# Tokens spread in pairs by products over half the rows, and inner products moved behind each search, in a PEER layer

## The reference, cut to what matters

```python
q = (x @ w_q).reshape(bsz, seq, 8, 2, 128)
s1 = einsum('bshd,hnd->bshn', q[..., 0, :], sub_k1)      # 128 scores for each token, head and half
s2 = einsum('bshd,hnd->bshn', q[..., 1, :], sub_k2)
v1, i1 = top_k(s1, 16); v2, i2 = top_k(s2, 16)
top_s, pos = top_k(all 256 sums v1 + v2, 16)             # 16 experts of 128*128, for each head
gates = softmax(top_s)
u = u_tab[experts]                                       # experts: 128 for each token
act = gelu(einsum('ced,cd->ce', u, x)) * gates
out = einsum('ce,ced->cd', act, v_tab[experts])
```

## Time and profile before

| | |
|---|---|
| median of three executions | 1939.52 us |
| profiled execution, its time / its span | 1947.71 / 1946.0 us |
| TensorE busy | 1806.9 us, 93% of the span |
| VectorE busy | 926.9 us, 48% |
| ScalarE busy, GpSimd busy | 432.9 us, 427.8 us (22% each) |
| moved by DMA | 620.29 MB, 319 GB/s over the span |
| TensorE's `spread_token` products in the window 1401.7 to 1619 | 192 |

### The profile page before, as it was taken

The page is one execution under the profiler, slowest core; times in us unless marked ns, Lnnn a source line. Parts: engine busy times, 40 slices in busy tenths (PEclk is TensorE's granted clock), DMA queues, the critical chain, the costliest instruction groups (busy, mean ns, idle before and its releaser), DMA issues. The chain is left out here.

```text
span 1946.0 us, 23689 instructions
## 1 busy us (share of the span) xinstructions
PE 1806.9 (93%) x9356; PEld 1190.3 (61%) x9356; DVE 926.9 (48%) x1988; ACT 432.9 (22%) x839; POOL 427.8 (22%) x312
## 2 busy tenths in 40 slices
PE   4989999988999999998899999979699999999998
PEld 4975444437787744442675548978588885444443
DVE  4467311123567731112798625966666662222222
ACT  5462111114345321111511424200100110000001
POOL 6820000015668400000300015112022121112110
PEclk7999899998999989999999999999899999999999
DMA  9886799994568589999432333699789999999996
GB/s 394 347 320 217 316 430 429 429 430 170 198 235 313 227 328 430 430 429 429 154 108 87 141 122 118 217 367 389 292 354 391 410 393 373 416 415 403 417 414 269
DMA packets 95089, 620.29 MB, mean 319 GB/s; under 512 B 11520, under 2 KB 12032, under 8 KB 60672
## 3 DMA queue, kind: packets, MB, share of 16 engines
q1 hardware_dynamic: 75824, 482.88, 62.5%
q0 software_dynamic: 18432, 134.23, 17.0%
q10 hardware_dynamic: 720, 1.61, 0.2%
HBM read 617.63 MB, written 1.05 MB: 318 GB/s over the span
## 5 line engine op out<-in xcount | busy, mean ns | idle before, releaser
L3038 PEld LDWEIGHTS bank<-peer_xT,peer_tiles_a 128*128 128x128 f32 x1376 | 160.3, 192 | 21.1 <-issue 12.5
L3038 PE MATMUL bank<-peer_xT,peer_tiles_a 128*128 128x128 f32 x1376 | 164.5, 276 | 6.7 <-DMA peer_tiles_a<-in_peer_u 4.6
L3087 PE MATMUL bank<-peer_tiles_a,peer_H 128*128 128x512 f32 x344 | 159.6, 602 | 6.2 <-DMA peer_tiles_a<-in_peer_v 4.2
L227 POOL TENSOR_TENSOR w_lo<-ring,w_hi 128x1024 fp32r<-128x1024 f32 x60 | 148.3, 2474 | 64.0 <-ACT w_hi L217 63.6
L3262 DVE CUSTOM_DVE_ANT_0 peer_junk<-peer_rows_b,bank 128x1024 bf16<-128x1024 f32 x64 | 78.1, 1220 | 166.8 <-issue 163.8
L1091 PE MATMUL bank<-ring,moe_slots 128*64 128x512 f32 x576 | 132.0, 609 | 9.7 <-DMA ring<-in_stream 9.7
L3058 PE MATMUL bank<-peer_x_rows_hi,peer_ident 128*128 128x512 f32 x256 | 130.6, 510 | 0.4 <-DVE peer_pre L3262 0.3
L3262 DVE CUSTOM_DVE_ANT_0 peer_junk<-peer_rows_a,bank 128x1024 bf16<-128x1024 f32 x48 | 58.6, 1220 | 123.6 <-issue 119.9
L3087 PEld LDWEIGHTS bank<-peer_tiles_a,peer_H 128*128 128x128 f32 x344 | 64.5, 191 | 82.6 <-issue 72.1
L3134 POOL DMA_INDIRECT peer_rows_a<-in_peer_uv,peer_index x48 | 45.5, 949 | 306.5 <-PE bank L3068 263.4
L3134 POOL DMA_INDIRECT peer_rows_b<-in_peer_uv,peer_index x64 | 60.3, 943 | 231.2 <-PE bank L3068 216.3
(11 more groups left out here) (518 smaller groups left out, 3591.6 us busy)
## 6 DMA issues: line engine op xcount, KB each, us to landing
ring<-in_stream SPq DMA_DIRECT2D x103, 2048.0 KB, 12.7
early<-in_stream SPq DMA_DIRECT2D x32, 2048.0 KB, 18.2
peer_tiles_a<-in_peer_u SPq DMA_DIRECT2D x86, 512.0 KB
peer_tiles_a<-in_peer_v SPq DMA_DIRECT2D x86, 512.0 KB
sb_mod_ring<-in_ada_t SPq DMA_DIRECT2D x64, 512.0 KB, 6.3
peer_tiles_b<-in_peer_u SPq DMA_DIRECT2D x42, 512.0 KB
peer_tiles_b<-in_peer_v SPq DMA_DIRECT2D x42, 512.0 KB
ret_mod_ring<-in_ada_t SPq DMA_DIRECT2D x32, 512.0 KB, 5.2
```

The lines of the kernel that those rows point to most:

```text
L227: pool.tensor_tensor(self.shaped(self.w_lo, q, by_columns), self.quarter(n, q, by_columns), self.shaped(self.w_hi, q, by_columns).bitcast( ...
L3038: last = pe.matmul(K.bank[:, 2 + n // 4 % 2, n % 4 * P:(n % 4 + 1) * P], u[:, k, :], xT[:, k, :], start=(k == 0), stop=(k == KD - 1))
L3087: last = pe.matmul(K.bank[:, 2 + dh, :], H[:, m, :], first.slot(n)[:, dh * 512:(dh + 1) * 512], start=(m == 0), stop=(m == PK - 1))
```

## The change

It does three things.

1. **Pairs.** `spread_token(i)` becomes `spread_pair(p)`, which spreads tokens 2p and 2p + 1 by eight products: each has 64 rows instead of 128 (the one-hot column and the token rows of one 64-row half), and the products of the two halves stand next to each other in the list and write different banks (4, 5 for one token, 6, 7 for the other). `token` is renumbered so that each pair has one token of each half.
2. **One set of banks.** A pair fills all of banks 4 to 7. So `spread_pair` waits until both `dot`s of the pair before are done; in the groups stretch each `gate_unit` waits for the `dot`s of the pair before it and the spread waits for `h_gated` of the units before it. The groups are written two at a time: 8 `keys`, 4 `gate_unit`s and 3 pairs.
3. **Places.** `pick_head` calls `dot_at` after each half and at its end, 24 places in all. From the sixth place (counted from 0: place 5) on, every second one runs two `dot`s. On TensorE the 20 tokens of this stretch stand after tiles 27, 30, ... 54 instead of 25, 27, ... 63. The exponential of the first tile (`PICKED_AT`) stands on ScalarE after tile 63 instead of tile 59.

```diff
-TOKENS_FROM = 24
-PICKED_AT = 59
+FIRST_TOKEN = 26
+PICKED_AT = 63
-BESIDE_PICKS = (EARLY - TOKENS_FROM) // 2
+BESIDE_PICKS = 20
+PAIR_AT = {FIRST_TOKEN + 1 + 3 * p: p for p in range(BESIDE_PICKS // 2)}
...
-    token = lambda i: P // QUAD * (i % QUAD) + i // QUAD
+    strip = lambda i: (0, 2, 1, 3)[i % QUAD]
+    token = lambda i: P // QUAD * strip(i) + i // QUAD
...
-            def spread_token(i):
-                if BESIDE_PICKS <= i <= VALUES_FROM + 1:
-                    pe.wait_ge(dotted, i)
-                elif i >= 2:
-                    pe.wait_ge(dotted, i - 1)
-                elif i == 1:
+            def spread_pair(p):
+                if p:
+                    pe.wait_ge(dotted, 2 * p)
+                else:
                     pe.wait_ge(index_made, 1)
-                one = first.ident[:, token(i):token(i) + 1].to_broadcast([P, P])
                 for dh in range(2):
                     for n, part in enumerate(first.x_rows):
-                        last = pe.matmul(K.bank[:, 4 + 2 * buffer_of(i) + dh, :], one, part[:, dh * 512:(dh + 1) * 512], start=(n == 0),
-                                         stop=(n == 1))
+                        for r in range(2):
+                            t, own = token(2 * p + r), slice(64 * r, 64 * (r + 1))
+                            last = pe.matmul(K.bank[:, 4 + 2 * r + dh, :], first.ident[own, t:t + 1].to_broadcast([64, P]),
+                                             part[own, dh * 512:(dh + 1) * 512], start=(n == 0), stop=(n == 1))
                 last.then_inc(spread, 1)
-                if i % QUAD == 1 and i > QUAD:
-                    values_of(i // QUAD - 1)
+
+            def weigh_pair(p):
+                if p % 2 == 0 and p:
+                    values_of(p // 2 - 1)
...
             def gate_unit(m):
                 pe.wait_ge(a_ready, m + 1)
                 pe.wait_ge(b_ready, m + 1)
+                pe.wait_ge(dotted, BESIDE_PICKS + 2 * (3 * (m // 4) + m % 4 // 2 + 1))
...
             turn_picks(0, 6)
+            pe.wait_ge(selT_made, 1)
+            for e in range(GROUPS_LEFT // 2):
+                n, m, p = EARLY + 8 * e, 4 * e, BESIDE_PICKS // 2 + 3 * e
+                spread_pair(p)
                 keys(n)
+                weigh_pair(p)
                 keys(n + 1)
+                gate_unit(m)
+                gate_unit(m + 1)
                 keys(n + 2)
+                pe.wait_ge(h_gated, m + 2)
+                spread_pair(p + 1)
...
             for m in range(PK):
-                for i in range(before_values(m), before_values(m + 1)):
-                    spread_token(VALUES_FROM + i)
+                for p in range(pairs_before(m), pairs_before(m + 1)):
+                    spread_pair(p)
                 values(m)
+                for p in range(pairs_before(m), pairs_before(m + 1)):
+                    weigh_pair(p)
...
+            def dot_at(place):
+                i = place + BESIDE_PICKS - 3 * PK_HEADS
+                if i > 0 and i % 2:
+                    dot(i - 1)
+                    dot(i)
```

More of the change, by code:

```diff
@@ L2963, in peer_stage, with pairs_before @@
     qT = S.first_tables[:].rearrange("p (h t) -> p h t", t=T)
-    def before_values(m):
-        return min(m * (TOKENS - VALUES_FROM) // (PK - 6), TOKENS - VALUES_FROM)
-    def buffer_of(i):
-        return 0 if BESIDE_PICKS <= i < VALUES_FROM else i % 2
+    def pairs_before(m):
+        return VALUES_FROM // 2 + min(m * ((TOKENS - VALUES_FROM) // 2) // (PK - 6), (TOKENS - VALUES_FROM) // 2)
     with nc.Block() as block:
@@ L3198, in _ @@
                     exponential(0)
-                if n % 2 == 1 and n > TOKENS_FROM:
-                    spread_walked((n - TOKENS_FROM) // 2)
-            for g in range(GROUPS_LEFT):
-                i = BESIDE_PICKS + 3 * g
-                spread_walked(i)
-                spread_walked(i + 1)
-                gelu(EARLY // 4 + g)
-                spread_walked(i + 2)
-            for i in range(VALUES_FROM, TOKENS):
-                spread_walked(i)
+                if n in PAIR_AT:
+                    pair_walked(PAIR_AT[n])
+            for e in range(GROUPS_LEFT // 2):
+                p = BESIDE_PICKS // 2 + 3 * e
+                pair_walked(p)
+                gelu(EARLY // 4 + 2 * e)
+                pair_walked(p + 1)
+                pair_walked(p + 2)
+                gelu(EARLY // 4 + 2 * e + 1)
+            for p in range(VALUES_FROM // 2, TOKENS // 2):
+                pair_walked(p)
             act.activation(warm[:], eps[:], ACT.Sqrt)
@@ L3225, in pick_head @@
                     top_sixteen(dve, c, val[:, half, :], idx[:, half, :], scores[:, tt, m * PK:(m + 1) * PK])
+                    dots_at(3 * h + half)
                 c.settle()
@@ L3306, in _ @@
             for h in range(PK_HEADS):
-                pick_head(0, h)
-                for i in range(max(h - 1, 0) * BESIDE_PICKS // (PK_HEADS - 1), h * BESIDE_PICKS // (PK_HEADS - 1)):
-                    dot(i)
+                pick_head(0, h, dot_at)
             recover(0)
```

70 lines of the change are left out of this document (37 added, 33 removed).

## The result

The changed kernel takes 1923.05 us in the median of four executions (1920.88 to 1923.89), the kernel before 1940.37 us in the median of four (1938.49 to 1945.17). The ratio is 0.9907, 95% interval 0.989 to 0.9925: a gain of about 17 us, 0.9%. The forecast was 1912.5 us, 27 us less, with a range of 1901 to 1930. The profiled execution took 1923.27 us, span 1921.6.

The account below looks back on a forecast made before the run. DMA at 416 GB/s was taken to bound late picks and nearly the values, TensorE the groups, with both idle at the gap. Gains of 8 (picks), 13 (groups) and 6 (values) sum to 27 us: 1939.5 to 1912.5, range 1901 to 1930.

Parts of the forecast that it names:

- The wait on the exponential: Before turn_picks: TensorE waits for gelu, table load, exponential, three small normalize steps and handovers, 3.4 us in all.
- 9 x 1.8 + 1.94 = 18.1: End of the picks: TensorE has nine tiles and a quad left from about 1372.0, until 1390.1.
- 1.20 forecast: Cost of a pair on TensorE: 0.96 us of side-by-side steps plus 0.24, against 2.04 for two tokens.
- The row on which the choice between rule and trace rested: Trace before: a 0.19 us weight load lies under a product on the same 128 rows, so loads were taken as hidden.
- I allow 0.75 us a round, 6 us: Groups: allowance for new waits of gates and pairs on VectorE, taken off the 20.4 us saving.
- Two groups ... After: 24.15 us: Groups: TensorE time for two groups falls from 26.7 to 24.15 us, 20.4 less in all.
- less stock left over from the groups takes 1.5: Values: less stock from the groups takes 1.5 us off the 7.5 us gain, leaving 6.
- some 15 us or more: Values: TensorE's added waits for peer_v tiles beyond the present ones, at 414 to 416 GB/s.
- Late gathers and waits eat the groups' gain: Rival: at 2.4 us of waits a round the groups gain nothing, time 1926; chance 0.13.
- The halves take turns: Rival: a pair takes 2.16 us, with 7 us of group waits, time 1950; chance 0.10 including loads that don't hide.
- DMA filled entirely: Rival: waits covered and stock sufficient, the 41 us bound is neared, time 1900; chance 0.07.
- the signs that were to show the forecast wrong: Pair over 1.6 us, TensorE waiting over 2 us a round for dotted or h_gated, values' DMA clearly below 410 GB/s.

Follow-up runs that it names:

- e1: Kernel before with only the new places (tokens after tiles 27, 30, ... 54, dot places, exponential after tile 63), spreads over 128 rows: 1935.31 us, ratio 0.9968.
- e5: Changed kernel with each of a pair's eight products over all 128 rows; places, waits and banks kept: 1934.99 us, ratio 0.9966.
- e10: Changed kernel with the exponential behind tile 59 and the groups' last quad summed ahead of the first v tile: 1921.47 us, ratio 0.9894.
- e8: Changed kernel with the last 30 pairs spread over 126 v tiles instead of 122: 1924.42 us, ratio 0.9921.
- e2: Changed kernel with the picks' old places (pairs after tiles 27, 31, ... 63, dots at ends of heads, exponential behind 59): 1932.15 us, ratio 0.9958.
- e3: Changed kernel with a pair's four products of one half issued before the four of the other: 1926.34 us, ratio 0.9921.
- e4: Changed kernel with the exponential back behind tile 59 instead of 63: 1920.79 us, ratio 0.9899.

## Why the prediction was right or wrong

The direction and the range were right, and the size was off: 17 us against 27. By the stretches 8 + 13 + 6 were forecast and 7.0 + 11.9 - 2.0 came.

**Picks: right in sum, with two errors that nearly cancel.** 8 forecast, 7.0 measured, and e1 shows that the places alone do it (6.6). The wait on the exponential was to be 3.4 us and is 3.35. TensorE ends its tiles at 1383.87, which is 120.0 us behind the first gather; forecast was 1390.1, 118.7 behind it. But the way there is another. The last pair ends 98.1 us behind the first gather instead of 100.6. The sum "9 x 1.8 + 1.94 = 18.1" counts a quad that isn't there: behind the last pair of the picks no quad falls due, the fifth one stands in the groups. And the nine tiles take 21.9 us, because TensorE waits for tiles three times, 1.64, 1.72 and 1.42 us, which the sum left out. So tiles that DMA brings set this end, and not TensorE's work; that the result is within 1.3 us is partly luck. Not forecast was the half clock behind so short a wait.

**The pair: 1.20 forecast, 1.12 on its own rows, and 1.39 with what it does to its neighbours.** A tile ahead of a pair takes 1.88 us, one ahead of a 128-row spread 1.71 (in e5 as in before); a tile behind a pair and ahead of a quad takes 1.98, behind a 128-row pair (e5) 1.88. So 0.17 us on the way in and 0.10 on the way out are paid in the tiles. I took the change of shape from the quad, whose 0.23 contains it, but counted it inside the pair's own steps, where only part of it is.

The row on which the choice between rule and trace rested held up. In after's timeline with weight loads a load for the lower part starts at 1401.52 and ends under the products that started at 1401.41 on the same rows:

```profile
1401.41 0.50 PE L3056 MATMUL bank<-peer_x_rows_hi,peer_ident 64*128 64x512 f32 x2
1401.52 0.19 PEld L3056 LDWEIGHTS bank<-peer_x_rows_lo,peer_ident 64*128 64x128 f32 x2
1401.74 0.39 PE L3056 MATMUL bank<-peer_x_rows_lo,peer_ident 64*128 64x512 f32 x2
```

The Trainium skill ("TensorE: Matmul & The Clock Gate", Part 3, The mechanism) says in one sentence that a load overlaps products in flight only when its row group differs. By that rule the pair would take 1.96 us; the trace shows 1.12, and the measurement decides. The same section, further up, also lets a load run ahead when it goes to the background weight buffer; this trace agrees with that, though it doesn't show where the load goes.

**Groups: nearly right in sum (13 and 11.9), with two errors that cancel.** The step "I allow 0.75 us a round, 6 us" for the new waits was wrong: TensorE shows none behind the first pair, and e5 with the same waits has the length of before. The step "Two groups ... After: 24.15 us" was too low by 0.78: a round takes 24.93. Of it the tiles are 1.90 instead of 1.80 on average (49.86 less six pairs of 1.12, eight gate units of 0.895 and three quads of 1.85 leaves 30.4 us for sixteen tiles), the gate units 0.895 instead of 0.81; pairs and quads are a little cheaper. I had read each kind in the one row where it was shortest, and the cost of coming back from another kind of product stands in the next tile. The half clock at the start of the stretch costs 2.2 us more (1388.74 to 1440.79 is 52.05 us for what later takes 49.86).

**Values: wrong, and this is the step that failed.** The prediction said that 124.6 MB at 416 GB/s take 299.5 instead of 307 us, 7.5 less, "less stock left over from the groups takes 1.5". Both halves of it fell: the 6 us of gain did not come.
- The 406 GB/s were not a rate a little too low all along, which a faster TensorE could have raised. They were 416 nearly throughout and three dips, the larger two at the entry and at the last slots. The faster TensorE left these two: 22.8 us of idle DMA in the stretch before, 22.1 after. The other profiles say the same: 20.3 and 20.2 in e1 and e5, which spread tokens over 128 rows, and 18.8 to 24.6 in the seven others with pairs and whole tiles of `v`. e10 moved the first dip without gain, e8 only moved some of the idle time at the end.
- The stock was worth more than 1.5. Groups and values move 208 MB together. The faster groups moved 1.0 MB less in their time, and the values had 1.1 MB more: 1.1 / 416 = 2.6 us. The same shows in e2, e3 and e8, whose groups moved 80.3 to 80.6 MB against 81.4 and 82.0 in e1 and e5.

Together -2.6 + 0.7 = -1.9 us, the -2.0 of the table. Since length is bytes over rate, this sum must come out; and 2.0 us is no more than the scatter between profiles, so what is shown is that the 6 us are missing, not that the values lost 2. This also puts the groups' 11.9 us in their true light: 9.5 us of them are idle DMA filled, 2.4 are bytes put off to the values. Over the layer the idle time fell by 7.0 + 9.5 + 0.7 = 17.2 us, nearly all of it in the picks and the groups. What the change gives TensorE in the values is waiting: 13.7 us less busy, 12.1 us more of waits for `v` tiles, a little under the forecast "some 15 us or more".

**The rivals.** "Late gathers and waits eat the groups' gain" had nearly the measured total (1926) by a mechanism that e5 excludes. "The halves take turns" is excluded by the 1.12 us; e5 is what it would have been but for the 7 us of waits that the rival counted: 0.9966, the gain of the places alone (e1 0.9968). "DMA filled entirely" fails at the dips and at the start of the groups. Of the signs that were to show the forecast wrong one came, if weakly: the values move 407 GB/s, less than 410, and not the 414 to 416 that the forecast named.

## What to carry to other kernels

Cut the stretch whose transfers bound it into pieces of 10 us before you count its missing bandwidth as something to win: an average of 406 against 416 GB/s was full rate with a few holes in it, and the faster engine filled none of the larger ones. Follow the bytes through the stages: where one stage runs faster without moving its share, the next one pays, and the gain is only the idle transfer time that is gone. When a product of another shape goes in, read its price from the period of the whole pattern, since a part of it stands in the products ahead and behind. And test each part of a change by itself: the one small move that looked harmless, the exponential four tiles later, seems to have cost time.

## What the runs showed of the hardware

- Products of 64 rows on the two halves of the array run side by side: two of 64x512 in one step of 0.23 us, where two of 128x512 take 0.46 (e5). It makes no difference whether the kernel's source interleaves the halves or has four of one and then four of the other (1.12 and 1.13 us); in both traces the products of the halves stand side by side.
- Between these and fp32 products over 128 rows a price shows outside of the pair: the tile ahead takes 1.88 us instead of 1.71, the tile behind 1.98 instead of 1.88.
- A wait of 3.35 us, followed by one of 0.65, left a granted clock of 0.69 in the 10 us behind the first; without the first (e4, where the one of 0.65 is still there) it was 1.00.
